# A two-block transformer kernel on one Trainium2 core: half of each weight residual is subtracted by GpSimd instead of VectorE

## What is computed

```python
# block 1: adaLN, windowed attention with sinks, SwiGLU
mod = silu(c) @ ada_w + ada_b
x = x + g1 * rmsnorm(windowed_gqa_sink(h, w_qkv, w_o, sink, rel_bias))
x = x + g2 * rmsnorm(swiglu(h2, ffn_w_in, ffn_w_out))
# block 2, layer 0: differential attention and a spatial gate, over a context of 256 more tokens
xs = layer_norm(alpha * xs + g1 * mixer_ab(hx, hc, ...))
xs = layer_norm(alpha * xs + g2 * peer(hx, wq, keys, u_tab, v_tab))
# block 2, layer 1: multiscale pooling, then peer again
```

## Time and profile before

| | us |
|---|---|
| runs | 2108.55, 2118.98, 2113.91 |
| median | 2113.91 |
| span of the profiled execution, first to last instruction | 2109.7 |
| time of the profiled execution itself | not recorded apart from its span |
| TensorE busy / VectorE busy / ScalarE busy / GpSimd busy in the span | 1777.2 / 1458.9 / 912.1 / 618.7 |
| the 130 subtractions of line 1570, all before 666 us | 94 from W and 36 from X or Y, median 1.22 each |

### The profile page before, as it was taken

The page is one execution under the profiler, slowest core; times in us unless marked ns, Lnnn a source line. Parts: engine busy times, 40 slices in busy tenths (PEclk is TensorE's granted clock), DMA queues, the critical chain, the costliest instruction groups (busy, mean ns, idle before and its releaser), DMA issues.

```text
span 2109.7 us, 22413 instructions
## 1 busy us (share of the span) xinstructions
PE 1777.2 (84%) x7293; PEld 1069.0 (51%) x7293; DVE 1458.9 (69%) x3032; ACT 912.1 (43%) x2383; POOL 618.7 (29%) x573
## 2 busy tenths in 40 slices
PE   4888999899988799997788777988998877777776
PEld 3757998798877454442232232455554422323222
DVE  6676867777776677766676767527677667677675
ACT  2446433534473344444444444424444444444443
POOL 1160000000001344443344333213454433443431
PEclk9988999999999999999999999999999999999999
DMA  9753668555566899999999999967999999999996
GB/s 369 283 200 120 259 224 317 200 200 202 198 220 200 338 421 420 421 421 419 420 421 422 421 421 422 369 219 294 416 418 421 421 421 421 421 421 421 421 422 258
DMA packets 114837, 723.80 MB, mean 343 GB/s; under 512 B 11520, under 2 KB 13360, under 8 KB 34208
## 3 DMA queue, kind: packets, MB, share of 16 engines
q0 software_dynamic: 74864, 540.30, 61.8%
q1 hardware_dynamic: 39856, 182.07, 23.6%
HBM read 721.24 MB, written 1.08 MB: 342 GB/s over the span
## 4 chain that ended last, share of the span: by engine, by line
DMA 38%; PE 33%; DVE 14%; ACT 7%; issue 5%; POOL 3%; SPq 0%; DVEq 0%; ACTq 0%; POOLq 0%
DMA X<-in_k_uv,EI 28%; PE PS L2254 11%; DMA Z<-in_k_uv,EI 8%; PE PS L1943 5%; PE PS L1945 4%; PE PS L1944 4%; DVE junk L1930 3%; PE PS L2230 3%; DVE ACC L1554 3%; POOL X L1067 2%; DVE WL L1570 2%; PE PS L2038 2%; DMA W<-in_ada_w 1%; ACT WH L1076 1%; PE PS L2271 1%
## 5 line engine op out<-in xcount | busy, mean ns | idle before, releaser
L2254 PE MATMUL PS<-X,dg 128*128 128x512 f32 x1380 | 666.5, 615 | 136.8 <-ACT dg L1076 135.3
L1930 DVE CUSTOM_DVE_ANT_0 junk<-H,X 128x1024 f32<-128x1024 f32 x345 | 421.7, 1222 | 245.0 <-DMA X<-in_k_uv,EI 235.0
L1067 POOL DMA_INDIRECT X<-in_k_uv,EI x345 | 371.0, 1075 | 515.7 <-PE PS L2254 324.7
L2254 PEld LDWEIGHTS PS<-X,dg 128*128 128x128 f32 x1380 | 248.6, 193 | 511.8 <-ACT dg L1076 301.8
L1076 ACT ACTIVATE CF<-DOT 128x1 f32<-128x1 f32 x512 | 103.6, 202 | 667.1 <-DVE DOT L1930 664.8
L2254 PE MATMUL PS<-Z,dg 128*128 128x512 f32 x480 | 234.3, 614 | 60.8 <-ACT dg L1076 60.5
L1076 ACT ACTIVATE dg<-CP,CG 128x128 f32<-128x128 f32 x512 | 205.5, 401 | 16.7
L1930 DVE CUSTOM_DVE_ANT_0 junk<-H,Z 128x1024 f32<-128x1024 f32 x120 | 146.7, 1223 | 92.5 <-DMA Z<-in_k_uv,EI 90.2
L2254 PEld LDWEIGHTS PS<-Z,dg 128*128 128x128 f32 x480 | 83.7, 190 | 193.7 <-ACT dg L1076 128.7
L1943 PE MATMUL PS<-XH,WH 128*128 128x256 f32 x592 | 175.8, 297 | 3.8 <-DVE WL L1570 2.2
L1944 PE MATMUL PS<-XL,WH 128*128 128x256 f32 x592 | 170.9, 289 | 0.0
(11 more groups left out here) (320 smaller groups left out, 2574.9 us busy)
## 6 DMA issues: line engine op xcount, KB each, us to landing
W<-in_ada_w SPq DMA_DIRECT2D x56, 1024.0 KB, 5.7
Y<-in_ada_w SPq DMA_DIRECT2D x16, 1024.0 KB, 6.2
W<-in_k_win SPq DMA_DIRECT2D x16, 1024.0 KB, 5.0
W<-in_k_ffi SPq DMA_DIRECT2D x13, 1024.0 KB, 6.2
Y<-in_k_ffi SPq DMA_DIRECT2D x9, 1024.0 KB, 4.9
W<-in_ffn_w_out SPq DMA_DIRECT2D x8, 1024.0 KB, 6.2
W<-in_peer_wq SPq DMA_DIRECT2D x8, 1024.0 KB, 13.2
W<-in_ab_w_out SPq DMA_DIRECT2D x6, 1024.0 KB, 5.2
```

What stands on the lines that cost most here:

```text
L1067: e.indirect_dma_start(out=WS[k][:, :], out_offset=None, in_=I[f"k_uv{ly}"][:, :], in_offset=bass.IndirectOffsetOnAxis(ap=EI[t][:, j:j + 1 ...
L1930: e.tensor_tensor_reduce(junk, H[:, t, :], d[:, 0:D], 1.0, 0.0, ALU.mult, ALU.add, DOT[:, j:j + 1]).then_inc(v_dot, 1)
L2254: p = e.matmul(PS[:, 2 * t + q, :], dgb[n % 4][:, :], d[:, D + q * 512:D + (q + 1) * 512], start=(j == 0), stop=(j == 127))
```

## The change

The first half of each low piece stays on VectorE and counts `v_lo` once for each part. The second half is emitted in GpSimd's walk through the plan, at the same step of the list, and counts the new semaphore `g_lo`. TensorE's `split_half` waits for the one or the other. `vacated` now returns a list, so that whoever reuses the buffer of a part waits for both. All 65 parts are treated alike.

```diff
             if kind == "ldw":
-                return v_lo, 2 * a[0] + 2
+                return [(v_lo, a[0] + 1), (g_lo, a[0] + 1)]
...
                     if before:
-                        w.wait_ge(*vacated(before))
+                        for s, count in vacated(before):
+                            w.wait_ge(s, count)
...
+                elif kind == "split" and a[1]:
+                    n = a[0]
+                    d = slot("ldw", n)[0]
+                    w.wait_ge(a_hi, 2 * n + 2)
+                    e.tensor_tensor(WL[n % 2][:, 1024:2048], d[:, 1024:2048], WH[n % 2][:, 1024:2048].bitcast(F32),
+                                    ALU.subtract).then_inc(g_lo, 1)
...
-                elif kind == "split":
-                    n, i = a
-                    d, arrived, count = slot("ldw", n)
-                    z = slice(1024 * i, 1024 * i + 1024)
-                    w.wait_ge(a_hi, 2 * n + i + 1)
-                    e.tensor_tensor(WL[n % 2][:, z], d[:, z], WH[n % 2][:, z].bitcast(F32), ALU.subtract).then_inc(v_lo, 1)
+                elif kind == "split" and a[1] == 0:
+                    n = a[0]
+                    d = slot("ldw", n)[0]
+                    w.wait_ge(a_hi, 2 * n + 1)
+                    e.tensor_tensor(WL[n % 2][:, 0:1024], d[:, 0:1024], WH[n % 2][:, 0:1024].bitcast(F32),
+                                    ALU.subtract).then_inc(v_lo, 1)
...
                 w.wait_ge(a_hi, 2 * n + i + 1)
-                w.wait_ge(v_lo, 2 * n + i + 1)
+                w.wait_ge(g_lo if i else v_lo, n + 1)
```

More of the change, by code:

```diff
@@ L819, in build @@
         d_gath = {k: sem(f"d_gath{k}") for k in RING}
-        g_init, g_an, g_gn8, g_own, g_fold = (sem("g_" + n) for n in ("init", "an", "gn8", "own", "fold"))
+        g_init, g_an, g_gn8, g_own, g_fold, g_lo = (sem("g_" + n) for n in ("init", "an", "gn8", "own", "fold", "lo"))
         (p_small, p_mod, p_xt, p_bias, p_part, p_y, p_as, p_at, p_ao, p_row, p_rope, p_ds, p_dt, p_do, p_gate, p_tt,
@@ L851, in vacated @@
             if kind == "ldw":
-                return v_lo, 2 * a[0] + 2
+                return [(v_lo, a[0] + 1), (g_lo, a[0] + 1)]
             if kind == "lda":
-                return v_ada, vada(a[0])
+                return [(v_ada, vada(a[0]))]
             if kind == "ldq":
-                return p_pq, nth.last_pq[a[0], a[1] // 2]
+                return [(p_pq, nth.last_pq[a[0], a[1] // 2])]
             if kind == "ga":
-                return p_dg, a[0] + 1
+                return [(p_dg, a[0] + 1)]
             if a[0] < 4:
-                return p_pi, nth("pi", 1, a[0] // 2, a[0] % 2)
+                return [(p_pi, nth("pi", 1, a[0] // 2, a[0] % 2))]
             if a[0] < 6:
-                return (p_band, 16) if a[0] == 4 else (p_grp, 16)
-            return (p_w, a[0] - 5) if a[0] < 9 else (p_po, 1)
+                return [(p_band, 16) if a[0] == 4 else (p_grp, 16)]
+            return [(p_w, a[0] - 5) if a[0] < 9 else (p_po, 1)]
         def last_in(k):
             return [name for name, place in where.items() if place[0] == k][-1]
-        y_free = [vacated(last_in(11)), vacated(last_in(12))]
+        y_free = vacated(last_in(11)) + vacated(last_in(12))
         ROWS = [(MC[0][:, 16:24], R[0], R[1][:, :], 0.0), (MC[0][:, 40:48], R[1], junk, 0.0),
```

## The result

The changed kernel takes **2136.99 us** (median of 4 runs, 2134.17 to 2138.88) against 2112.78 (2108.55 to 2118.98) for the kernel before, run beside it: a ratio of 1.0112, 95% interval 1.0096 to 1.0128. Taken together the change costs about 1.0%, 21 us. Forecast were 2129 us and "slower".

What follows compares the result with a forecast made beforehand. It took TensorE to bound FI, with VectorE's round 0.2 us short of it, and the subtraction to be partly on the second attention's path. 2 - 4 + 12.5 + 0 - 1 + 5 = +14.5 on 2113.9 gave 2129 us, range 2106 to 2147.

Steps and rivals of the forecast that it cites:

- The exclusion and the turn: VectorE operations with two SBUF inputs stand still 2.2 us while GpSimd reads; the engine that waits longer goes first.
- FI: Feed-forward input: VectorE's round grows from 11.3 to 13.4 us against TensorE's 11.5, seven times; +12.5 us.
- The clock: TensorE's granted clock may fall after stalls in the feed-forward input; nothing put in the sum, upper bound there +17.
- FO and the stages behind 665 us: FO: 0.25 us more per part, hidden by halves made ahead, 0, at most +2; from 665 us no subtraction runs.
- norms before IN: One pair of subtractions there is followed by work from PSUM: -1 us.
- Start and first attention: Start to 77 us: two pairs grow by 1.06, +2; first attention: four second halves leave VectorE's queue, -4.
- Second attention and AO: 19 pairs cost +12 us of VectorE's time, 11 of 19 on the path: +7, taken as +5.
- the step with the exponentials that the forecast had counted: Second attention: ten of 19 pairs have a sum or two exponentials behind them, costing up to 1.06 us each.
- the gain of 1.14 where the row maximum from PSUM follows: Second attention: three of 19 pairs are followed by that maximum with WH just ready, -1.14 us each.
- Nothing blocks: Rival: GpSimd's subtraction does not hold VectorE, so work leaving it gains 11 us, 2103 us; chance 0.12.
- VectorE wins the turns: Rival: GpSimd runs in VectorE's waits, feed-forward input loses only +2, the others cancel, 2116 us; chance 0.22.
- More than the hold: Rival: clock falls in half the feed-forward stalls, second attention +11, start +4, or longer GpSimd operation; 2145 us; chance 0.16.

Runs made afterwards that it cites:

- e1: Changed kernel with the second halves of parts 12 to 28 (feed-forward input) back on VectorE: 2120.89 us, ratio 1.0044.
- e9: Kernel before, with GpSimd subtracting only the second halves of parts 12 to 28: 2123.93 us, ratio 1.0055.
- e11: The changed kernel once more, unaltered, on another occasion with a second profiled execution: 2130.91 us, ratio 1.0089.
- e2: Changed kernel with the second halves of parts 46 to 64 (second attention and its output) back on VectorE: 2121.3 us, ratio 1.0046.
- e10: Kernel before, with GpSimd subtracting only the second halves of parts 6 to 11 (first attention and its output): 2107.91 us, ratio 0.9979.
- e8: Changed kernel with the second halves of parts 6 to 11 back on VectorE: 2137.97 us, ratio 1.0136.
- e4: Kernel before, plus an idle two-input GpSimd subtraction of 128 x 896 at parts 12 to 28: 2128.25 us, ratio 1.0086.
- e5: Kernel before, plus an idle one-input GpSimd multiplication of 128 x 896 at parts 12 to 28: 2122.34 us, ratio 1.0049.
- e6: Kernel before, plus an idle GpSimd fill of 128 x 896 with zeros at parts 12 to 28: 2112.24 us, ratio 1.0005.

## Why the prediction was right, step by step

**The exclusion and the turn** held as worked from the earlier trace rows: a hold of 2.16 us (2.2 forecast), GpSimd's operation 2.35 undisturbed (2.35 taken, from the earlier trace rows; the rounded output costs nothing there either), VectorE's 1.14 saved for 2.16 to 2.20 lost.

**FI: right in its parts.** Forecast were a round of 13.4 us, seven stalls and +12.5. Seen were 13.54, seven, and 13.7 in the marks; e1 and e9 put it at 12 by the medians. The clock, at which nothing was put because VectorE is the later of the two, fell behind none of the seven stalls of the first trace. Where it fell with another late round behind it (twice in e11, three times in e9) it cost nothing, as forecast; at the end of the seven rounds of e11 it cost 5 us.

**FO and the stages behind 665 us: 0, as forecast**: marks 29 and 45 are equal (in e11 1.1 apart), and the last stretch is 1445.1 us against 1444.7. The -1 of the norms before IN wasn't seen: the first trace is at +14.0 at part 45 and at +14.6 at part 46. The forecast had work from PSUM behind the pair there; in the trace the GpSimd halves of 419.26 and 427.23 us each hold a small subtraction of line 1474 on SBUF tiles, by 1.2 and 1.75 us.

**Start and first attention: +2 and -4, the sum right.** Over the four traces that share the changed kernel's code up to part 12 (the changed one, e11, e1, e2) the mark there is -1.7 in the mean, and +0.3 over the five that share the code of before: -2.0, where the forecast had 2 - 4. e10 puts the second term at -4.4. One mechanism of the start was missed. By the marks at part 5 the start alone is +1.7 in the mean of the changed kernel's traces (that one, e11, e8, e1, e2) and +0.6 in those of the kernels with the start of before: about +1, so that the attention's share is about -3 by the traces. The first held operation at the start is not one with two inputs from SBUF:

```profile
50.14 3.43 DVE L1559 TENSOR_SCALAR ACC<-W,CS 128x2048 f32<-128x2048 f32 x1
```

Alone it takes 1.28 us for 2048 columns, half the time of the sums with two, and it was held for 2.15.

**Second attention and AO: the term that was mis-sized.** "Together [...] +12 us of VectorE's time, of which 11 of 19 lie on the path: +7; I take +5." The 12 was right. In the trace the 19 GpSimd subtractions from 438 to 690 us stretch the VectorE operations beside them by 33.0 us in all (each held duration less the shortest of its kind), and 19 x 1.14 = 21.7 left the queue: +11.3. The share was wrong. From part 45 to 64 the marks grow by 10.3 (8.7 in e11), e2 gives back 11.5, and the kernels that have no GpSimd half here (e2, e4, e5, e6, e9, e10) take 1.1 to 2.1 us **less** for this stretch than the one trace of before, so that practically all of the 11.3 reached the end. The chain of waits had put the subtraction's rows on the path 11 times in 19; but the held operation is another one than the one that was on the chain: it is what follows. That this is why the share failed is my reading of the traces; no run changes it alone. The chain from 438 to 689 us of the changed kernel, which answers to the earlier trace rows:

```profile
by line: DVE ACC L1562 16.7%; issue 13.6%; PE PS L1951 7.9%; PE PS L1952 7.2%; PE PS L1953 7.2%; DVE st L1727 5.3%; ACT E L1084 4.3%; PE PS L2046 4.0%; ACT WH L1084 3.6%; DVE st L1739 3.1%; DVE WL L1577 3.0%; ACT L1084 2.0%; DVE st L1729 1.
```

The subtraction fell from 10.4% to 3.0%, as one would wish, and its place was taken by "issue" (8.4 to 13.6%), the sums (14.6 to 16.7%) and L1739, the factor by which two exponentials are combined, which the row of before does not name. "Issue" is time for which the trace names no wait. Its longest pieces in the chain are these two,

```profile
499.33 3.10 issue
548.29 3.09 issue
```

and the first lies inside VectorE's own half of 499.08, which stands still there, as its timeline shows:

```profile
496.82 2.35 DVE L1562 SCALAR_TENSOR_TENSOR ACC<-W,CS,ACC 128x2048 f32<-128x2048 f32 x1
499.08 3.42 DVE L1577 TENSOR_TENSOR WL<-W,WH 128x1024 fp32r<-128x1024 f32 x1
...
510.45 2.05 DVE L1739 SCALAR_TENSOR_TENSOR st<-st 128x1 f32<-128x1 f32 x1
```

The 12 itself came out of a different make-up. Only 3 of the 19 held a sum, and ten held small operations on the statistics (L1739 and L1729 four times each, L1752, L1760), by 0.9 to 2.2 us each. Four of these, L1739, stand in the step with the exponentials that the forecast had counted, but it is the operation of 128 x 1 that is held and not the large one. And the gain of 1.14 where the row maximum from PSUM follows didn't come:

```profile
482.92 1.22 DVE L1727 TENSOR_REDUCE st<-PS 128x2 f32<-128x1024 f32 x1
484.17 1.11 DVE L1729 TENSOR_SCALAR st<-st 128x2 f32<-128x2 f32 x1
```

The maximum passes undisturbed, but the scaling behind it takes 1.11 us instead of 0.17, so that 0.2 of the 1.14 is left.

**The rivals.** "Nothing blocks" (2103) and "VectorE wins the turns" (2116) fall by the timeline and by both sets of runs. "More than the hold" (2145) had two of its parts true: the clock in e11, and the second attention at 11. The sum with that one term corrected is 2 - 4 + 12.5 - 1 + 11.3 = +20.8, beside the 21 measured. That it fits to a few tenths is luck: the -1 wasn't seen, the start was +1 and FI 12 to 13.7, and the two sets differ by 5 us. In the forecast itself 2113.9 + 14.5 is 2128.4, not 2129.

**Left open.** Which of the parts 6 to 11 make e10's gain wasn't tried one by one, nor whether a piece smaller than a half, moved in FI, would fit into VectorE's waits of 0.76 and 0.26 us.

## What to carry to other kernels

Before work goes from VectorE to GpSimd, look at what VectorE does next: if an operation that GpSimd's reads hold starts while GpSimd is still at work, 1.14 us moved away costs up to 2.2 of standing still, however small that operation is. One operation from PSUM in between isn't enough if such a small one follows it. Where VectorE would idle anyway (the first attention, where it waited for ScalarE), the move pays. The same edit gained 4 us in six parts and cost some 25 in the others, so make such a choice part by part. And a stage that is bounded by another engine can still lose: FI's TensorE had 0.2 us in a round to spare, and 2.2 came.

## What had not been expected of the hardware

- **The hold doesn't depend on the size of the held operation**, but on how much of GpSimd's is left when it starts. Operations on 128 x 1 to 128 x 4 float32 that take 0.15 to 0.22 us alone took 2.05 to 2.32, and 1.10 where they came 1.4 us behind GpSimd's start.
- **One input from SBUF was held too** in TENSOR_SCALAR operations: L1559, 1.28 us alone for 2048 columns (the sums with two inputs take 2.34), 3.43 beside GpSimd, and L1752, on 128 x 4, 2.32 instead of 0.17. The Trainium skill, "SBUF — State Buffer", section "Who interferes with whom", has it that such an operation of one tensor and scalars can enter a mode that takes both ports and so contends; the rows agree in that it is held. Not every operation with one input is: the RECIPROCAL of 128 x 1 at 464.73 us (L1736) took 0.14 us, as alone, beside a GpSimd half that then held L1739.
- **How long GpSimd holds depends on what it reads**: per 896 columns 1.49 us with two inputs, 0.73 with one, 0 for a fill. The one-input operation itself is the longer one beside VectorE's pair (median 2.54 us against 1.77), so GpSimd's own duration does not tell the price.
- **After the same stall of 2.27 us the granted clock fell or did not**: 0.50 in the kernel before and in e11, 1.00 in e9. It fell behind one of 1.79 us in e11 too, and behind none of the six of 1.78 in the first trace. Where nothing else is late, such a stretch costs 1.6 us or more in one execution, which is more than a third of what the first attention gains, and only medians over many runs got beneath it.
